# Last head of a stick-breaking attention and the first output units: low halves on VectorE, high halves on GpSimd, new orders, second unit in banks of its own

## What is computed

```python
z = einsum('bhqd,bhkd->bhqk', q_blk, k) * scale
log_fail = where(mask, log_sigmoid(-z), 0.0)
after = cumsum(log_fail, axis=3, reverse=True) - log_fail
w = where(mask, exp(log_sigmoid(z) + after), 0.0)
out = einsum('bhqk,bhkd->bhqd', w, v)
...
y = concatenate([y_sb, y_lru], axis=-1)      # 16 chunks of 128 features
h = h + einsum('bse,ed->bsd', y, w_out)      # "out3"
```

## Time and profile before

| | us |
|---|---|
| median of 3 executions | 2208.73 (2207.75 to 2211.65) |
| the profiled execution | 2211.55 |
| its span, first to last instruction | 2209.8 |
| PE busy | 2170.0 |
| DVE busy | 1444.8 |
| ACT busy | 969.1 |
| POOL busy | 137.8 |

### The profile page before, as it was taken

The page is one execution under the profiler, slowest core; times in us unless marked ns, Lnnn a source line. Parts: engine busy times, 40 slices in busy tenths (PEclk is TensorE's granted clock), DMA queues, the critical chain, the costliest instruction groups (busy, mean ns, idle before and its releaser), DMA issues. The chain is left out here.

```text
span 2209.8 us, 31171 instructions
## 1 busy us (share of the span) xinstructions
PE 2170.0 (98%) x10148; PEld 1792.1 (81%) x10148; DVE 1444.8 (65%) x2633; ACT 969.1 (44%) x1893; POOL 137.8 (6%) x161
## 2 busy tenths in 40 slices
PE   8999999999999999999999999999999999998999
PEld 6878888888788888888888788888888888887787
DVE  6677777777643567777777833576767676767432
ACT  5444444444432435555555633444443444355221
POOL 0100000000211010000000122200000000002000
PEclk9999999999999999999999999999999999999999
DMA  7312222224624623332222553532333233324542
GB/s 214 95 53 81 81 81 81 81 81 122 190 77 113 184 77 86 85 85 83 83 83 80 179 157 82 178 95 77 107 88 107 76 107 88 107 76 148 176 138 66
DMA packets 371007, 234.45 MB, mean 106 GB/s; under 512 B 4884, under 2 KB 345108, under 8 KB 370966
## 3 DMA queue, kind: packets, MB, share of 16 engines
q1 hardware_dynamic: 368838, 229.74, 36.4%
q10 hardware_dynamic: 2128, 4.19, 0.5%
HBM read 209.80 MB, written 24.12 MB: 106 GB/s over the span
## 5 line engine op out<-in xcount | busy, mean ns | idle before, releaser
L596 PE MATMUL pp<-act_hi,w_hi 128*128 128x512 f32 x2400 | 957.9, 399 | 17.4 <-DVE act_lo L820 9.9
L598 PE MATMUL pp<-act_hi,w_lo 128*128 128x512 f32 x2400 | 939.5, 391 | 0.0
L597 PE MATMUL pp<-act_lo,w_hi 128*128 128x512 f32 x2400 | 938.3, 391 | 0.0
L570 DVE TENSOR_TENSOR w_lo<-raw,w_hi 128x512 fp32r<-128x512 f32 x676 | 460.7, 709 | 330.9 <-ACT w_hi L561 328.2
L561 ACT ACTIVATE w_hi<-raw 128x512 fp32r<-128x512 f32 (+1 forms) x692 | 404.8, 620 | 351.6 <-PE pp L598 190.5
L596 PEld LDWEIGHTS pp<-act_hi,w_hi 128*128 128x128 f32 x2400 | 452.5, 189 | 114.5 <-DVE w_lo L570 13.3
L598 PEld LDWEIGHTS pp<-act_hi,w_lo 128*128 128x128 f32 x2400 | 452.1, 188 | 97.7
L597 PEld LDWEIGHTS pp<-act_lo,w_hi 128*128 128x128 f32 x2400 | 452.9, 189 | 92.2 <-issue 4.1
L1765 ACT ACTIVATE s_prob<-ps,s_minus 128x256 f32<-128x256 f32 x128 | 59.4, 470 | 84.5 <-DVE s_minus L1843 79.5
L1131 ACT ACTIVATE prob<-ps,minus,q_scale 128x512 f32<-128x512 f32 (+1 forms) x64 | 39.0, 615 | 96.8 <-DVE minus L1193 96.8
L596 PE MATMUL pp<-c_hi,w_hi 128*128 128x512 f32 x192 | 76.6, 399 | 3.4 <-DVE square L1231 1.4
(11 more groups left out here) (365 smaller groups left out, 2618.4 us busy)
## 6 DMA issues: line engine op xcount, KB each, us to landing
raw<-w_in SPq DMA_DIRECT2D x48, 1024.0 KB, 5.8
raw<-swa_w_in SPq DMA_DIRECT2D x36, 1024.0 KB, 5.6
raw<-mla_w_in SPq DMA_DIRECT2D x23, 1024.0 KB, 5.8
raw<-mla_w_out SPq DMA_DIRECT2D x16, 1024.0 KB, 6.6
raw<-swa_w_out SPq DMA_DIRECT2D x16, 1024.0 KB, 6.4
raw<-w_out SPq DMA_DIRECT2D x16, 1024.0 KB, 7.6
raw<-mla_w_ukv SPq DMA_DIRECT2D x16, 512.0 KB, 4.4
x_feature_major<-xT SPq DMA_DIRECT2D x8, 1024.0 KB, 8.5
```

Of the source, the lines that this page charges most:

```text
L570: q.eng.tensor_tensor(dst, raw_piece(tile, p), high, ALU.subtract).then_inc(s_lo, 1)
L596: q.eng.matmul(psum[:, :], wh, ah, start=start and n == 0, stop=False)
L597: q.eng.matmul(psum[:, :], wh, al, start=False, stop=False)
L598: last = q.eng.matmul(psum[:, :], wl, ah, start=False, stop=stop and n == PIECE // P - 1)
```

## The change

It does seven things.

1. `Y_GPSIMD[3]` becomes empty: the low halves of chunks 0 to 7 in the third layer go from GpSimd to VectorE. GpSimd makes instead the high halves of chunks 8 to 14 (`tensor_copy`, with a semaphore of its own).
2. The first unit of `out3` is split in the order `FIRST_ORDER`, in which the two tiles alternate; slots, counts and `raw_free` follow it. `raw_free` of tile 0 of unit 1 in `out3` becomes base + 7, since piece (0, 3) has index 6; it was base + 4.
3. In the last head VectorE has an order written out by hand: pieces and y chunks in the order in which TensorE uses them; `y_lo` of chunks 12 to 14 stands ahead of the steps of block 1; the low part of v (`v_lo_e`), `pt_lo3_e` and `pt_lo2_e` come between the blocks.
4. TensorE does five early pieces ahead of `turn(3)` in place of four, one between `turn(3)` and `turn(2)`, and the first three chunks of m = 6 ahead of `turn(1)`.
5. ScalarE loses `y_hi` of chunks 8 to 14 and makes the pieces in the new order; `pt_hi2_e` follows `pt_hi3_e`.
6. Unit 1 of every output phase adds up in `ps[0]` and `ps[2]`, and TensorE no longer waits for `x0` and `x1` of unit 0.
7. The first `SECOND[n]` pieces of unit 1 (5, 5 and 6) are split ahead: ScalarE and VectorE do them after the attention phase and before the halves of y chunk 15.

```diff
-Y_GPSIMD = {1: range(0, 8), 2: range(4, 8), 3: range(0, 8)}
+SECOND = {1: 5, 2: 5, 3: 6}
+Y_GPSIMD = {1: range(0, 8), 2: range(4, 8), 3: range(0, 0)}
...
+FIRST_ORDER = [(0, 0), (0, 1), (1, 0), (1, 1), (0, 2), (1, 2), (0, 3), (1, 3)]
+def first_order(phase, k, p):
+
+    return FIRST_ORDER.index((k, p)) if phase == "out3" else PIECES * k + p
...
         if self.phase in OUTPUTS and isinstance(self.i, int) and self.i == 1:
-            return self.base() + PIECES * (self.k + 1)
+            return self.base() + first_order(self.phase, self.k, PIECES - 1) + 1
...
-                q.eng.activation(act_hi[:, j, :], y_chunk(n, j), ACT.Copy).then_inc(s_yhi, 1)
+                if n == LAYERS and j in range(8, KC - 1):
+                    q.eng.tensor_copy(act_hi[:, j, :], y_chunk(n, j)).then_inc(s_yhi_g, 1)
+                else:
+                    q.eng.activation(act_hi[:, j, :], y_chunk(n, j), ACT.Copy).then_inc(s_yhi, 1)
...
+        def output_bank(i, k):
+
+            return ps[2 * k] if isinstance(i, int) and i == 1 else pp[k]
...
-                if p == 0:
+                if p == 0 and not (isinstance(i, int) and i == 1):
                     before(k)
...
+        def second_unit(q, n, part):
+
+            for m in range(SECOND[n]):
+                part(q, Tile(f"out{n}", 1, m % 2), m // 2)
...
                 early_output(q, 3, 0, 1)
                 q.eng.wait_ge(*q.at("V.gate"))
-                early_output(q, 3, 1, 4)
+                early_output(q, 3, 1, 5)
...
             turn(3, None)
...
-                early_output(q, 3, 4, 5)
+                early_output(q, 3, 5, 6)
             turn(2, None)
             if not proj:
-                early_output(q, 3, 5, 6)
-            turn(1, "V.pt_lo3")
+                early_output(q, 3, 6, 7, range(3))
+            turn(1, f"V.pt_lo3{moved}")
             piece(Q3, 2, pp[0])
-            turn(0, "V.pt_lo2")
+            turn(0, f"V.pt_lo2{moved}")
...
+            if not proj:
+                for m in (1, 2, 3):
+                    first_piece(m, lo)
+                y_lo(q, 3, range(4, 8))
+                first_piece(4, lo)
+                y_lo(q, 3, range(8, 12))
+                q.eng.wait_ge(*q.at("A.ln3"))
+                weights_log(3)
+                values_lo(i - 1, "v_lo_e")
+                first_piece(5, lo)
+                q.eng.wait_ge(*q.at("A.ln2"))
+                weights_log(2)
+                turned_lo(3)
+                first_piece(6, lo)
+                first_piece(7, lo)
+                y_lo(q, 3, range(12, 15))
+                q.eng.wait_ge(*q.at("A.ln1"))
+                weights_log(1)
+                turned_lo(2)
+                q.eng.wait_ge(*q.at("A.ln0"))
+                weights_log(0)
+                silu_s("silu_e", "A.tanh_e")
...
             pipelined(q, swa_V, "swa", Tile("out2", 0, 0))
-            y_lo(q, 2, range(12, KC))
+            y_lo(q, 2, range(12, KC - 1))
+            second_unit(q, 2, lo)
+            y_lo(q, 2, range(KC - 1, KC))
             output_V(q, 2)
...
             pipelined(q, stick_V, "stick", Tile("out3", 0, 0))
+            second_unit(q, 3, lo)
             y_lo(q, 3, range(KC - 1, KC))
             output_V(q, 3)
...
-            y_lo(q, 3, Y_GPSIMD[3])
+            y_hi(q, 3, range(8, KC - 1))
```

More of the change, by code:

```diff
@@ L272, in piece_slot @@
                                            or self.phase not in OUTPUTS else SPLIT)
-        for first in reversed(FIRST_OUTPUT_PIECES):
+        for phase, first in reversed(list(zip(OUTPUTS, FIRST_OUTPUT_PIECES))):
             if n >= first + SPLIT:
                 k, p = (n - first) % 2, (n - first) % SPLIT // 2
-                n = first + PIECES * k + p
+                n = first + first_order(phase, k, p)
         return n % SPLIT
@@ L1368, in unit @@
                     p, k = divmod(m, 2)
-                    hi(q, Tile(phase, i + 1, k), p)
+                    if not (isinstance(i, int) and i == 0 and m < SECOND[n]):
+                        hi(q, Tile(phase, i + 1, k), p)
                     if n < LAYERS and p == PIECES - 1:
@@ L1407, in unit @@
                         x_V(q, n, i, k)
-                    if not last:
+                    if not last and not (first and m < SECOND[n]):
                         lo(q, Tile(phase, i + 1, k), p)
@@ L1426, in output_V @@
             q.eng.wait_ge(s_xload, 16 * n)
-            if n == 1:
-                unit(1)
-            with loop(q.eng, 2 if n == 1 else 1, LAST) as i:
+            unit(1)
+            with loop(q.eng, 2, LAST) as i:
                 unit(i)
@@ L2140, in hi_, with first_piece @@
                     for p in pieces:
-                        hi(q, t_, p)
+                        if t_.phase == "out3":
+                            first_piece(p, hi)
+                        else:
+                            hi(q, t_, p)
+            def first_piece(m, part):
+                k, p = FIRST_ORDER[m]
+                part(q, Tile("out3", 0, k), p)
             def turned_hi(b, step=None):
@@ L2156, in stick_A @@
                 y_hi(q, 3, range(4, 8))
-                for p in range(3):
-                    hi(q, Tile("out3", 0, 1), p)
+                first_piece(4, hi)
             if attn:
@@ L2183, in stick_A @@
             if not proj:
-                y_hi(q, 3, range(8, 12))
+                for m in (5, 6, 7):
+                    first_piece(m, hi)
             if attn:
@@ L2258, in lo_, with first_piece @@
                     for p in pieces:
-                        lo(q, t_, p)
+                        if t_.phase == "out3":
+                            first_piece(p, lo)
+                        else:
+                            lo(q, t_, p)
+            def first_piece(m, part):
+                k, p = FIRST_ORDER[m]
+                part(q, Tile("out3", 0, k), p)
             def col(name, k=0):
@@ L2336, in stick_V @@
             lo_(K3, 0)
-            turned_lo(3)
+            if proj:
+                turned_lo(3)
             lo_(K3, 1)
-            turned_lo(2)
+            if proj:
+                turned_lo(2)
             turned_lo(1)
@@ L2402, in stick_V @@
                 sub_lo(q, d_k_lo[:, :], d_k[:, :], d_k_hi[:, :], "k_lo")
-            lo_(6, 0, 1, 2, 3)
-            if proj:
-                q.eng.wait_ge(*q.at("A.v_hi"))
-                sub_lo(q, d_v_lo[:, :], pt[0][:, :], d_v_hi[:, :], "v_lo")
+            if proj and nxt.phase == "out3":
+                y_lo(q, 3, range(0, 4))
+                lo_(6, 0)
+            else:
+                lo_(6, 0, 1, 2, 3)
+                if proj:
+                    values_lo(i, "v_lo")
         block = ctx.enter_context(nc.Block())
@@ L2433, in _ @@
             pipelined(q, mla_A, "mla", Tile("out1", 0, 0))
-            y_hi(q, 1, range(12, KC))
+            y_hi(q, 1, range(12, KC - 1))
+            second_unit(q, 1, hi)
+            y_hi(q, 1, range(KC - 1, KC))
             output_A(q, 1)
@@ L2438, in _ @@
             pipelined(q, swa_A, "swa", Tile("out2", 0, 0))
-            y_hi(q, 2, range(12, KC))
+            y_hi(q, 2, range(12, KC - 1))
+            second_unit(q, 2, hi)
+            y_hi(q, 2, range(KC - 1, KC))
             output_A(q, 2)
@@ L2451, in _ @@
             pipelined(q, mla_V, "mla", Tile("out1", 0, 0))
-            y_lo(q, 1, range(12, KC))
+            y_lo(q, 1, range(12, KC - 1))
+            second_unit(q, 1, lo)
+            y_lo(q, 1, range(KC - 1, KC))
             output_V(q, 1)
```

86 lines of the change are left out of this document (42 added, 44 removed), and 6 rows, old and new, of the table STEPS.

## The result

The changed kernel takes 2220.85 us in the median of four executions (2219.44 to 2221.47), the kernel before 2208.24 on the same occasion: a ratio of 1.005, 95% interval 1.0038 to 1.0062. It is slower, by 8 to 14 us. The profiled execution of after took 2221.29 us with a span of 2219.5, 9.7 more than the span of before.

The account below looks back on a forecast made before the run. TensorE was taken as the bound, busy 2170.0 us (98%). 7.2 us up to unit 1 of out3 plus 2.1 in out2 gave 9.3 us: 2220.9 for a profiled execution, median 2218.0, range 2208.5 to 2223.

Parts of the forecast that it names:

- The load that moves: Last head: y load of chunks 12 to 14 issued at 2033.1, 15 us later; TensorE stands 11.4 us.
- The second unit split ahead: In out3, VectorE's six low pieces (3.6 us) delay chunk 15; with the head, unit 1 starts 7.2 us later.
- In `out2`: Second output phase: five VectorE pieces make TensorE stand 2.5 us at chunk 15; less 0.44 saved, +2.1 us.
- ScalarE's pieces are free: Ahead of chunk 15, ScalarE's high pieces fit into its former idle time of 6.15 us and cost nothing.
- In `out1`: First output phase: a 1.6 us stand, covered by the 4.82 us wait for the load of x; cost 0.
- The copies' disturbance: Last head: GpSimd's first four high-half copies delay VectorE's y lows by 2.0 us in all.
- third rival: GpSimd's copies to fp32r cost 1.3 to 1.7 each, +3 us: 2221; slow copies or clock had chance 0.10.
- The total: Whole kernel: 7.2 us up to unit 1 of out3 plus 2.1 in out2, 9.3 us slower.
- what it moves, the end moves: From unit 1 of out3 TensorE runs without a gap, so a shift of its start shifts the end equally.
- clock that I had counted as 0: Half-clock stretches after TensorE's stands: one more long one costs +1 to +3, none saves 1.5; taken as 0.
- The offset: Profiled execution of before lay 2.8 us above its median, so 2220.9 profiled became a median of 2218.0.
- The fourth rival: The stands of 3.06, 3.03 and 3.38 us simply go, and half a slow stretch: 2199 us; chance 0.04.

Follow-up runs that it names:

- e1: The changed kernel with the third layer's load of y chunks 12 to 14 issued ahead of the load of tile 0 of unit 1: 2213.55 us, ratio 1.0015.
- e10: The kernel before with the third layer's load of y chunks 12 to 14 issued behind both tiles of unit 1: 2210.25 us, ratio 1.0001.
- e4: The changed kernel with no pieces of unit 1 split ahead in the first and second layers: 2219.37 us, ratio 1.0042.
- e2: The changed kernel with VectorE's low pieces of unit 1 behind the low half of y chunk 15 in all three layers: 2219.15 us, ratio 1.0045.
- e7: The changed kernel with 44 more matmuls on TensorE between turn(2) and the first product with chunk 12, result unused: 2222.19 us, ratio 1.0061.
- e3: The changed kernel with the edits of e1 and e2 together: 2209.73 us, ratio 0.9999.
- e5: e3 with TensorE's unit 2 waiting for x0 and x1 of unit 0 only, no longer for those of unit 1: 2205.73 us, ratio 0.9986.
- e8: The kernel before with only unit 1's own banks and first pieces split ahead, VectorE's behind chunk 15; old last head: 2209.13 us, ratio 0.9996.
- e9: e8 with TensorE's unit 2 waiting for x0 and x1 of unit 0 only: 2204.17 us, ratio 0.9976.

## Why the prediction was right

It gave 2218.0 in a range of 2208.5 to 2223; 2220.85 came. The mechanism held. That the sum met the profiled execution so closely is in part luck, as the points below add up.

- **The load that moves** was the step that decided, and it holds in each link: issue of the y load at 2035.84, that is 2032.7 counted from the old m = 0, where 2033.1 was forecast; 7.9 us to land where 8.9 was taken; a stand of 10.48 where 11.4 was forecast. e1 shows it by undoing it, e10 shows that there was slack which hid it before, at least 4 us of the 7 that were read.
- **The second unit split ahead** in `out3`: `y` to unit 1 took 7.4 us (2055.69 to 2063.13), forecast 6.3; the difference is half clock in the last six matmuls (2.4 us in place of 1.4). +7.6 for head and start together where +7.2 stood.
- **In `out2`** a stand of 2.40 (2.5 forecast) came, and e4 and e2 show that it comes from the pieces. Its price was mis-sized: a slow clock stretch followed it, about 1.7 us, which I had left out. It isn't certain to come: in e7, whose `out2` is the same, the clock stayed at 1.00 behind the same stand and chunk 15 to unit 1 took 3.5 us, not 5.1. That ScalarE's pieces are free holds in `out3` alone: in `out2` they cost 0.95 us once VectorE's are out of the way (e2). Together with the earlier finish of `out1` this gives the 3.15 us by which m = 0 is later: -0.6 at the end of the second attention (y lows of 12 at 1262.77 against 1263.35), +3.7 in `out2`.
- **In `out1`** nothing from the stand, as forecast: the load of x covers its 1.48 us. The -0.6 above is the clock behind it, less a new 1.04 us at unit 2; neither was forecast.
- **The copies' disturbance**, taken as 2.0 between 0 and 2, was 1.6. In after the copies took 0.62 alone and at most 1.07 beside the lows; the third rival's 1.3 to 1.7 was too high. The prediction says that no row shows such a copy, but the trace of before has some: line 1941 copies 128x512 to fp32r on GpSimd, in 0.62 or 0.67 us for most, and for the first two, beside VectorE's lows, 1.23 and 1.08, while five of those took 4.06 in place of 3.09 (807.05 and 807.18). Who loses differs from run to run. In e7, with the head of after, the first copy took 3.13 us while VectorE's lows kept their 0.6, and VectorE lost 1.7 us behind it. The Trainium skill's rule on the shared port (SBUF — State Buffer, "Who interferes with whom") agrees: y lows with two SBUF inputs went from 0.6 to between 0.9 and 1.1 us while GpSimd copied out of SBUF. The length of the copy is not what it states.
- **The total.** Measured it is +7.6 in the head, +3.7 in `out2`, -0.6 in `out1` and -1.1 behind unit 1: 9.6, forecast 9.3. The last term contradicts "what it moves, the end moves": unit 1 starts 10.8 us later and the span is 9.7 longer, because the slow stretch behind unit 1, 3.2 us at 0.56 in before, ended 1.3 us behind unit 1 in after. So the 2.0 us too little in head and `out2` were met by 1.7 us of clock that I had counted as 0. That is luck.
- **The offset.** The sum was right for the profiled execution (2220.9 forecast, 2221.29 measured) and 2.9 too low for the median. I took 2.8 off because the profiled execution of before lay that far over its median. After's lies 0.4 over its own. With 15 to 27 executions the kernel before has a median of 2209.3 to 2210.9, so a part of the 2.8 was chance of three executions. What the clock costs in the median isn't shown.
- **The fourth rival** ("all gains") was not only beaten by the six pieces. e3 has neither the load nor the pieces in the way and still gained nothing, for the wait at unit 2, which no rival of mine had.

What stays open: the sizes of single steps below 2 us, which these intervals can't separate; what GpSimd's copies alone cost, since no run takes them alone out of the changed kernel; and how far the clock, which differs between executions of one kernel, moves the medians.

## What to carry to other kernels

A load hangs on its place in the queue. When a counter that gates one transfer is raised, list what is issued behind it on the same queue and who waits for that, here a wait of 8.55 us on VectorE for a load that nobody had felt before. Work put ahead of a late operand is only free on an engine that waits there, and only while it fits into the wait: ScalarE's pieces did in `out3` and left 0.95 us in `out2`, VectorE's stood between the last result and the operand for which TensorE waited. And when a unit gets banks of its own, follow the old wait one unit on: unit 2 uses the banks of unit 0, its wait for unit 1 protected nothing, and dropping it was worth 3 to 5 us (e3 to e5, e8 to e9); no version that kept it was faster than the kernel before.

## What was not expected of the hardware

A GpSimd copy of 128x512 from float32 to fp32r took 0.62 us alone, as long as the float32 to float32 copy of before (0.61), and mostly 1.07 beside VectorE's lows; in e7 and e3 the first one took 3.13 and 3.72 us beside lows that were not slowed.

The clock behind a like stand differs between executions. The stand before m = 1 (3.06 us in before) was followed by full clock there, 1.00 in 2020 to 2029; in e9 and e10, with the same order in the head and stands of 2.99 and 2.71, it was 0.81 in those 9 us. That cost them nothing: TensorE came later to `turn(1)` and waited there 1.6 us in place of 3.03, and `turn(1)` came at the same distance from m = 0 (23.9 us in before, 23.8 in e9). But in before, behind the longer wait, the clock fell to 0.59 (2041 to 2044), and in e9 and e10 it stayed at 1.00, so that `turn(1)` to step `y` took 6.5 us in before and 4.9 in the two. Filling a stand of 10 us with 44 matmuls kept the clock at full through it, and the half clock came in `pv` instead.
